# Second block of a two-block network: attention regrouped in units of two heads, with the top-k rounds between the units

## The reference, cut to what matters

```python
# 8 heads of 64 over 2 key/value heads; 8 index heads of 32; top 128 of the 512 keys per query
def block(i):                                   # a block of 128 queries; four of them
    rel = relu(einsum('bthd,bsd->bths', qi_b, ki))
    isc = einsum('bths,bth->bts', rel, wi_b * idx_scale)
    isc = where(causal, isc, -inf)
    _, sel = top_k(isc, 128)
    s = einsum(q, k[sel]) * 64 ** -0.5          # only the selected keys count
    s = where(valid, s, -inf)
    return einsum(softmax(s), v[sel])
short_conv = sc_b * causal_dwconv(sc_c * u, w_conv)      # three taps, width 512, from three products of h
```

## Time and profile before

| | before |
|---|---|
| median of three runs | 4325.65 us |
| lowest, highest | 4324.61, 4326.67 us |
| the profiled execution's own time | 4326.43 us |
| its span, first to last instruction | 4324.6 us |
| granted PE clock over the span, share of full | 0.958 |
| busy share PE, DVE, ACT, POOL | 92%, 44%, 36%, 29% |

### The profile page before, as it was taken

One profiled execution on the slowest core, in us unless ns is written; L12 is line 12 of the kernel. 1 busy time (PEld: TensorE's weight loads), 2 busy tenths in 40 slices (PEclk: granted clock), 3 DMA queues, 4 the chain that ended last, 5 costly groups with the idle time before them and its releaser, 6 DMA issues.

```text
span 4324.6 us, 60899 instructions
## 1 busy us (share of the span) xinstructions
PE 3957.5 (92%) x25712; PEld 3124.9 (72%) x25712; DVE 1884.7 (44%) x2939; ACT 1565.4 (36%) x2376; POOL 1250.8 (29%) x765
## 2 busy tenths in 40 slices
PE   7988899999999799999788899999997889999998
PEld 6955678888776568877566677788775667777886
DVE  3265332323345533436955422334368554223333
ACT  4356222222355533332353333333323433333332
POOL 2011422222111133332222235333322222354332
PEclk9998899999999899999899999999998999999999
DMA  5013133322111022221101022222211010222222
GB/s 200 30 56 137 59 112 103 108 102 101 61 49 61 20 81 88 98 69 68 54 30 36 22 78 98 81 88 102 83 61 52 30 36 22 83 93 78 98 93 73
DMA packets 61358, 323.55 MB, mean 75 GB/s; under 512 B 6176, under 2 KB 6304, under 8 KB 36256
## 3 DMA queue, kind: packets, MB, share of 16 engines
q1 hardware_dynamic: 61088, 319.65, 21.1%
HBM read 317.53 MB, written 2.10 MB: 74 GB/s over the span
## 4 chain that ended last, share of the span: by engine, by line
PE 77%; DVE 12%; ACT 5%; POOL 3%; issue 2%; DMA 1%; SPq 0%; DVEq 0%; ACTq 0%; POOLq 0%
PE ps L1509 51%; PE ps L704 3%; PE ps L724 3%; PE ps L2544 2%; PE ps L338 1%; PE ps L1008 1%; PE ps L3018 1%; PE ps L1043 1%; DMA adab<-in_wada 1%; DVE ar L2303 1%; DVE small L2299 1%; PE ps L2623 1%; PE ps L1023 1%; PE ps L1025 1%; PE ps L2636 1%
## 5 line engine op out<-in xcount | busy, mean ns | idle before, releaser
L1481 POOL TENSOR_TENSOR PWL<-ring,PWH 128x1024 fp32r<-128x1024 f32 (+2 forms) x116 | 267.1, 2303 | 715.7 <-ACT PWH L1467 715.7
L1888 DVE SCALAR_TENSOR_TENSOR ftmp<-ps,vec,ftmp 128x511 f32<-128x511 f32 (+2 forms) x440 | 301.8, 695 | 356.1 <-ACT ftmp L1842 231.4
L1467 ACT ACTIVATE PWH<-ring 128x1024 fp32r<-128x1024 f32 (+2 forms) x216 | 211.7, 982 | 513.5 <-PE ps L1509 485.7
L1481 POOL TENSOR_TENSOR WL<-ring,WH 128x1024 fp32r<-128x1024 f32 (+3 forms) x102 | 227.1, 2227 | 581.9 <-ACT WH L1467 565.4
L1467 ACT ACTIVATE WH<-ring 128x1024 fp32r<-128x1024 f32 (+3 forms) x160 | 158.8, 994 | 641.5 <-PE ps L1509 639.7
L1509 PE MATMUL ps<-FH,WH 128*128 128x512 f32 (+1 forms) x1056 | 332.0, 369 | 18.7 <-POOL FL L1682 14.6
L1509 PE MATMUL ps<-FL,WH 128*128 128x512 f32 (+1 forms) x1056 | 325.8, 363 | 0.0
L1509 PE MATMUL ps<-FH,WL 128*128 128x512 f32 (+1 forms) x1056 | 325.7, 363 | 0.0
L1481 POOL TENSOR_TENSOR PW3L<-ring,PW3H 128x1024 fp32r<-128x1024 f32 (+2 forms) x92 | 210.8, 2291 | 289.0 <-ACT PW3H L1467 288.7
L1474 DVE TENSOR_TENSOR PWL<-ring,PWH 128x1024 fp32r<-128x1024 f32 (+2 forms) x100 | 125.5, 1257 | 353.6 <-ACT PWH L1467 353.6
L1509 PEld LDWEIGHTS ps<-FH,WH 128*128 128x128 f32 x1056 | 178.0, 192 | 67.3 <-issue 28.1
(11 more groups left out here) (566 smaller groups left out, 10004.8 us busy)
## 6 DMA issues: line engine op xcount, KB each, us to landing
ring<-in_wup SPq DMA_DIRECT2D x88, 1024.0 KB, 4.8
adab<-in_wada SPq DMA_DIRECT2D x56, 512.0 KB, 5.5
ring<-in_wgate SPq DMA_DIRECT2D x24, 1024.0 KB, 4.8
ring<-in_wdown SPq DMA_DIRECT2D x24, 896.0 KB, 4.7
ring<-in_win SPq DMA_DIRECT2D x18, 1024.0 KB, 4.8
ring<-in_wout SPq DMA_DIRECT2D x16, 1024.0 KB, 4.9
ring<-in_wada SPq DMA_DIRECT2D x14, 1024.0 KB, 5.3
ring<-in_wdown SPq DMA_DIRECT2D x12, 1024.0 KB, 4.9
```

Of the source, the lines that this page charges most:

```text
L1467: e.activation(wh, view, ACT.Copy).then_inc(*whi_a.up(L, n))
L1481: e.tensor_tensor(wl, view, wh.bitcast(F32), SUB).then_inc(*wlo_g.up(L, n))
L1888: e.scalar_tensor_tensor(out=dst, in0=src, scalar=conv_cols(L, ch, a), in1=dst, op0=MUL, op1=ADD).then_inc(*(ffn_v.up(L, "tap", x, j, c) i ...
```

## The change

Part by part:

- Queries Q are scaled by -0.125 as they leave PSUM, so that scores are negative and the softmax needs the minimum, without a scaling of it.
- Index heads: no masked copies. A head's product uses its own 32 rows of PE (four heads in four banks). Their weighted sum is made by PE: POOL writes eight diagonal matrices of the heads' weights (`DI`), and eight 128x128 products add up in one bank (`weighted`). ACT copies the sum out.
- Attention units are 16, of two heads and one row group. The scores of the two heads use 64 rows of PE each, in two banks; mask, minimum and reciprocal are one DVE instruction for both. The exponentials aren't scaled; the turn is a product with a diagonal of the reciprocals (`diag2`, written by POOL). The values of the two heads use 64 columns each and are copied out together. The copies of the turned weights are ACT's, except one of two for the last row group.
- The convolution has one bank (6) instead of two, ACT copies all its products to SBUF, and it is cut in halves of 12 matmuls.
- `attend2_plan` writes out 25 slots; a row of it is (index scores, sum, unit, halves, rounds, selection): which index group, which sum, which unit, which halves of the convolution, which rounds and which selection stand in each. Rounds of one row group stand behind each other, beginning while the other groups' scores are still made, and go on between units 0 to 10; selections stand in the slots of units 3, 6 and 10.

`units_at(s)` gives a slot's unit u, the one before it, t = u-1, and v = u-2. ACT's order in a slot is: the weight split of an even half, the copy of the index sum, the relus, the two exponentials of u, the weight copies of t, the copy of the convolution's product when an odd half has ended it, the copy of v's result. POOL's is: the eight diagonals at the first scores of a row group, the two diagonals of t (they wait for its reciprocal), the low part of the weights of an even half. In `masked(u)` DVE adds the mask to the two heads' scores from PSUM and takes the minimum; `conv` is the product, the three taps and the last product of the convolution.

```diff
-                e.tensor_copy(x, bank(p % 2)).then_inc(*lin_v.up(L, p))
+                if P_Q <= p < P_K:
+                    e.tensor_scalar(x, bank(p % 2), -0.125, None, MUL).then_inc(*lin_v.up(L, p))
+                else:
+                    e.tensor_copy(x, bank(p % 2)).then_inc(*lin_v.up(L, p))
...
+        def attend2_plan():
+
+
+            rows = [((1, 0), 0, None, 1, {}, 0), ((1, 1), 0, None, 1, {}, 0), ((2, 0), 1, None, 1, {}, 0), ((2, 1), 0, None, 1, {1: 3}, 0),
+                    ((3, 0), 2, None, 1, {1: 3}, 0), ((3, 1), 0, None, 1, {1: 2, 2: 2}, 0), (None, 3, None, 1, {1: 2, 2: 2}, 0)]
+            rounds = [{1: 2, 2: 2}] * 3 + [{2: 2}] + [{2: 2, 3: 2}] * 2 + [{3: 2}] + [{3: 3}] * 3 + [{3: 1}] + [{}] * 7
+            for s in range(18):
+                rows.append((None, 0, s if s < 16 else None, (2, 1, 2, 1, 2, 1, 2, 2, 1, 1, 1, 1)[s] if s < 12 else 0, rounds[s],
+                             {3: 1, 6: 2, 10: 3}.get(s, 0)))
...
         def tensor_attend2(e, w, L):
+            def index(qi, j):
...
+                for r in range(4):
+                    rows = slice(32 * r, 32 * r + 32)
+                    e.matmul(bank(r)[:, 0:n], QI[rows, j, qi * 128:qi * 128 + 128], KI[rows, 0, 0:n], start=True,
+                             stop=True).then_inc(*idx_mm.up(L, qi, 4 * j + r))
+
+            def weighted(qi):
...
+                for h in range(8):
+                    w.wait_ge(idx_a.at(L, "relu", qi, h))
+                    mm = e.matmul(isc_bank(qi)[:, 0:n], DI[:, h, :], relu_buf(h)[:, 0:n], start=h == 0, stop=h == 7)
+            def conv_half(y):
+                x, h = divmod(y, 2)
...
+                w.wait_ge(whi_a.at(L, n), low_ready(L, n))
+                if x:
+                    w.wait_ge(idx_a.at(L, "conv", x - 1))
+            def scores(u):
...
+                w.wait_ge(soft_v.at(L, u - 2, "masked") if u >= 2 else idx_a.at(L, "relu", 3, 7))
+                for a in range(2):
+                    rows = slice(64 * a, 64 * a + 64)
+                    mm = e.matmul(scores2(u)[:, a, 0:n], Q[rows, jt, qi * 128:qi * 128 + 128], KK[rows, kv, 0:n], start=True, stop=True)
+            def turn(u):
+                w.wait_ge(diag_g.at(L, u))
+                for a in range(2):
+                    w.wait_ge(soft_a.at(L, u, "exp", a), weights_taken(L, u - 1, a) if u else idx_a.at(L, "isc", 3 if a else 2))
+                    for b in range(ATT2[u][0] + 1):
+                        mm = e.matmul(bank(4 + a)[:, b * 128:b * 128 + 128], E2(u)[:, a, b * 128:b * 128 + 128], diag2(u)[:, a, :],
+                                      start=True, stop=True)
+            def values(u):
...
+                for b in range(qi + 1):
+                    for a in range(2):
+                        mm = e.matmul(bank(7)[64 * a:64 * a + 64, 0:128], VT[:, b, c:c + 64], weights2(u, a)[:, b * 128:b * 128 + 128],
+                                      start=b == 0, stop=b == qi)
+            for s, (sc, acc, _, halves, _, _) in enumerate(PLAN2):
+                u, t, v = units_at(s)
+                if acc:
+                    weighted(acc)
+                if sc:
+                    index(*sc)
+                if u is not None:
+                    scores(u)
+                for y in halves[0:1]:
+                    conv_half(y)
+                if t is not None:
+                    turn(t)
+                for y in halves[1:]:
+                    conv_half(y)
+                if v is not None:
+                    values(v)
...
         def vector_attend2(e, w, L):
+            for s, (sc, acc, _, halves, rounds, sel) in enumerate(PLAN2):
+                u, t, v = units_at(s)
+                if t is not None:
+                    w.wait_ge(soft_a.at(L, t, "exp", 1))
+                    e.reciprocal(stat2(t)[2], stat2(t)[1]).then_inc(*soft_v.up(L, t, "inv"))
...
+                if u is not None:
+                    masked(u)
+                for y in PLAN2[s - 1][3] if s else ():
+                    if y % 2:
+                        conv(y // 2)
+                for qi, it in rounds:
+                    largest(qi, it)
+                if sel:
+                    selection(sel)
+                if t is not None and ATT2[t][0] == 3:
+                    w.wait_ge(turn_mm.at(L, t, 0), pv_mm.at(L, t - 2))
+                    e.tensor_copy(weights2(t, 0), bank(4)).then_inc(*wt_v.up(L, t, 0))

```

More of the change, by code:

```diff
@@ L2101, in gpsimd_turned @@
             pipeline([unit(p, *u) for p, u in enumerate(turned_units(L))])
[L2104 to L2112, removed]
-        def conv_bufs(ft):
-            return tmp2(14 + 2 * (ft % 2)), tmp2(15 + 2 * (ft % 2))
@@ L2117, in conv_fed @@
[L2117 to L2159, removed]
@@ new lines, in program, with relu_buf, isc_bank, conv_of @@
+        DI = hcf[:, 1024:2048].rearrange("p (h c) -> p h c", h=8)
+        ATT2 = [(qi, jt) for qi in range(4) for jt in range(4)]
+        def relu_buf(h):
+            return tmp2(6 + h)
+        def isc_bank(qi):
+            return bank(4 + qi % 2)
+        def conv_of(x):
+            return x // 3, (2, 0, 1)[x % 3]
+        def conv_bufs(ft):
+            return tmp2(14 + 2 * (ft % 2)), tmp2(15 + 2 * (ft % 2))
+        def conv_to(x):
+            ft, nm = conv_of(x)
+            return Y2[:, 4 + ft, :] if nm == 1 else conv_bufs(ft)[0 if nm == 2 else 1]
@@ new lines, in attend2_plan @@
+        def attend2_plan():
[5 more added lines that the diff above has]
+                             {3: 1, 6: 2, 10: 3}.get(s, 0)))
+            out, h, done = [], 0, {1: 0, 2: 0, 3: 0}
+            for sc, acc, u, halves, rnd, sel in rows:
+                todo = []
+                for i in range(max(rnd.values(), default=0)):
+                    for qi in sorted(rnd):
+                        if i < rnd[qi]:
+                            todo.append((qi, done[qi]))
+                            done[qi] += 1
+                out.append((sc, acc, u, list(range(h, h + halves)), todo, sel))
+                h += halves
+            assert h == 24 and all(x == 16 for x in done.values()), (h, done)
+            return out
@@ new lines, in program, with units_at, E2, weights2 @@
+        PLAN2 = attend2_plan()
+        def units_at(s):
+            first = next(i for i, x in enumerate(PLAN2) if x[2] == 0)
+            return [u if 0 <= u < 16 else None for u in (s - first, s - first - 1, s - first - 2)]
+        def E2(u):
+            return ar[:, 16472 + 1024 * (u % 2):17496 + 1024 * (u % 2)].rearrange("p (a c) -> p a c", a=2)
+        def weights2(u, a):
+            return tmp2(10 + 2 * (u % 2) + a)
+        def diag2(u):
+            return ar[:, 21592 + 256 * (u % 2):21848 + 256 * (u % 2)].rearrange("p (a c) -> p a c", a=2)
@@ L2345, in unit @@
-                yield 1
-                yield 1
-                w.wait_ge(turn_mm.at(L, u))
-                if u >= 2:
-                    w.wait_ge(pv_mm.at(L, u - 2))
-                e.tensor_copy(tmp2(6 + u % 2)[:, 0:n], bank(3 + u % 2)[:, 0:n]).then_inc(*wt_v.up(L, u))
-                yield 1
-            conv = vector_conv(e, w, L, (0, 1, 2))
-            among_scores(scores(), conv)
-            among_largest(largest(), conv)
-            first = selection()
-            next(first)
@@ L2358, in vector_attend2 @@
[L2358 to L2381 removed]
+                    w.wait_ge(soft_a.at(L, u - 8, "exp", 1))
```

319 lines of the change are left out of this document (147 added, 172 removed).

## The result

| | before | after |
|---|---|---|
| median | 4325.52 us (4 runs, 4324.61 to 4326.67) | 4288.94 us (4 runs: 4283.99, 4284.46, 4293.43, 4295.02) |
| profiled execution, its span | 4326.43, 4324.6 us | 4284.46, 4282.2 us |
| granted PE clock over the span | 0.958 | 0.961 |

The ratio is 0.9916, 95% interval 0.9899 to 0.9933: faster by 36.6 us. The forecast was 4285. The time is right; several of the reasons for it are not, as the trace shows.

What follows compares the result with a forecast made beforehand. The prediction had neither DVE nor PE full throughout, with DVE leading nearly all of slots 0 to 11 after the change. Stage 39.6 + 113.6 + 5 + 3 = 161.2 us against 181.8 and 182.1; 4326.4 - 41.5 = 4285 us, range 4252 to 4320.

Steps and rivals of the forecast that it cites:

- DVE's spread bounds the gain: Whole stage: neither DVE nor PE full throughout before; after, DVE leads nearly all of slots 0 to 11, 83.6 us.
- First part: Seven slots without units: PE works 38.8 us, first matmul 0.8 us in, DVE half idle; 39.6 us.
- Slots 0 to 11: Slots with units and rounds: DVE's 83.6 us plus its waits and the stalls beside POOL.
- The couplings: DVE's waits: 0.5 us for first scores, 4.0 at slot 0, 1.3 at slot 4, 1.7 at slot 11; 7.5 us.
- The stalls beside POOL: DVE's convolution products and selections beside POOL's weight splits: three stalls, 5 us a stage on top of unhindered times.
- Slots 12 to 15 with their clock loss: Last units, without rounds: a loop of 4.4 us a unit, 17.6 us, plus 3 us for PE at half clock.
- The tail: Behind the last unit: diagonal, turn, copy, values and copy with nothing beside; 4.9 us.
- The clock: PE stops 5.9 us at slot 10, then two slots at half speed: +3 us; gaps near 3 at slots 3 and 6 free.
- Signs named ahead: Trace signs: DVE busy near 118 us a stage, slots near 11 us at selections of groups 2 and 3, one half-clock stretch.
- Rival 3: Index path and units: PE tiles run in turn, not side by side; 4314 us, chance 0.05.
- rival 2: Units: DVE and PE wait alternately, hiding only half of PE's 81 us; stage 178, program 4318 us, chance 0.12.
- rival 4: Unit part: long DVE slots cost PE its clock throughout; stage 201, program 4365 us, slower than before, chance 0.07.
- Rival 1: Whole stage: no POOL stalls, no clock loss, slot 0's wait hidden; 150 to 153 us, program 4264, chance 0.14.

Runs made afterwards that it cites:

- e6: Changed kernel with only the plan edited: no rounds in the first seven slots, then 16 gathered slots of rounds, then units; stages 182.8 and 182.7 us.
- e1: Changed kernel with DVE's convolution step moved behind the rounds of its slot; stages 158.6 and 158.7 us, ratio to before 0.9905.
- e8: Changed kernel with the weighted sum over index heads moved from PE back to DVE; stages 165.5 and 165.5 us, ratio to before 0.9935.
- e2: Changed kernel with ACT's copy of a convolution product ahead of the exponentials where the finishing half is the slot's first; stages 162.5 and 162.6 us.
- e4: Changed kernel with all index heads on PE's rows 0 to 31, one row tile; stages 182.6 and 183.3 us, ratio to before 1.0002.
- e7: Changed kernel with both heads' scores on rows 0 to 63 and values of head 0 before those of head 1; stages 170.9 and 170.9 us.
- e3: Changed kernel with the edits of e1 and e2 together; stages 153.4 and 153.3 us, median 4260.7 us, ratio to before 0.9858.
- e10: e3 with more rounds of row groups 1 and 2 moved into the part without units; stages 150.7 and 150.7 us, ratio to before 0.9874.

## Why the prediction was right, and where not

- **That DVE's spread bounds the gain: right.** e6 gives back the whole 16 us a stage when the rounds are gathered again; e1 shows that what is taken from DVE in the units reaches the end nearly whole (100.7 to 92.2 us of busy time, 8.0 of the stage).
- **First part, 39.6 forecast, 43.0 measured.** Three terms make the 3.4 us. The first index product stood 1.7 us in, not 0.8. The six groups took 5.2 us from start to start, where the estimate was 3.9. Seven halves took 20.9, not 19.5: six of them 2.90 to 2.96 each instead of 2.78, and the last, behind the sum, 3.26. The longer halves are no sign of a change of tiling, which the prediction put at nothing "on an engine that is not the limit": in the kernel before a tile of 24 between products on all 128 rows took 5.74 us (3207.36 to 3213.10) instead of 5.57, which is as much more. PE is the limit of this part, though, and I had weighed its total of 121 us against DVE's 113, and not where each lies. The sum of the heads on PE cost little by that: 1.1 us a stage by e8.
- **Slots 0 to 11, 96.1 forecast with couplings and stalls, 97.7 measured** (2052.8 to the reciprocal at 2150.46). The couplings, 3.43 + 2.51 + 0.78 + 1.37 = 8.1 us, met the 7.5. Three came at slots 0, 4 and 11 as named; the 0.78 before the mask of unit 8 wasn't named, and the 0.5 for the first scores didn't come. The stalls beside POOL, put at 5, were five instructions and 8.9 us: this term was too small by 3.9. What was left of DVE's own work was 2.9 less than counted, although 2.7 us of it are rounds left over from the first part (the first mask stands at 2055.51). The last two errors nearly cancel.
- **Slots 12 to 15 with their clock loss, 20.6 forecast, 20.1 measured, by other terms.** DVE's timeline of the changed kernel at the end:

```profile
2153.11 1.23 DVE L2317 TENSOR_TENSOR ar<-ps,ar 128x1024 f32<-128x1024 f32 x1 [2.48 <-PE ps L2220]
...
2157.17 0.17 DVE L2375 RECIPROCAL small<-small 128x2 f32<-128x2 f32 x1 [0.99 <-ACT ar L2277]
...
2161.35 0.17 DVE L2375 RECIPROCAL small<-small 128x2 f32<-128x2 f32 x1 [0.99 <-ACT ar L2277]
...
2166.11 0.17 DVE L2375 RECIPROCAL small<-small 128x2 f32<-128x2 f32 x1 [0.99 <-ACT ar L2277]
...
2170.51 0.17 DVE L2375 RECIPROCAL small<-small 128x2 f32<-128x2 f32 x1 [0.99 <-ACT ar L2277]
```

  Reciprocals are 4.2 to 4.8 us apart, 4.45 on the mean, where 4.4 was forecast. The one before (2150.46 to 2157.17) is 6.71, with the wait of 2.48 for scores that stood behind a turn at half clock. The tail was 5.9, not 4.9.
- **The clock: the step that failed as it was put.** I had read from the earlier trace rows that gaps of 5.0 and 8.9 us bring 1.2 GHz, put one such stretch behind the gap at slot 10, and said of slots 3 and 6 that gaps near 3 cost nothing. The trace of the kernel before didn't bear that out. PE was at 1.2 GHz before the gap of 8.92 began, from 3.6 us into the one of 4.78 ahead of it (timeline of PE, then table by stretch):

```profile
3294.55 0.48 PE L2229 MATMUL ps<-cst,ar 128*128 128x128 f32 x1 [4.78 <-ACT ar L2264]
```

```profile
3292.00:3293.00 1.00, 0.00 (x0) 0.00 (x0) 0.41 (x4) 0.72 (x3) 0.00 (x0) 1.00 0.00 0
3293.00:3294.00 1.00, 0.00 (x0) 0.00 (x0) 0.90 (x5) 1.00 (x2) 0.13 (x1) 0.59 0.03 8
```

  In the changed kernel PE fell four times in the first stage, with gaps of 2.55, 4.31, 3.38 and, at slot 10, 4.77 us (and kept its clock in e2 after 1.78). The unit part has 0.92 granted, with PE at 1.2 GHz in several short stretches. Two parts of the changed kernel that hold such places, from the table by stretch:

```profile
2109.80:2119.80 10.00, 6.62 (x24) 5.36 (x23) 9.76 (x17) 1.75 (x6) 2.94 (x2) 0.72 0.13 29
2084.00:2094.00 10.00, 4.75 (x13) 3.76 (x14) 9.16 (x24) 2.46 (x8) 3.37 (x3) 0.66 0.18 54
```

  Much of it hid behind DVE. What reached DVE can be read at two places: 1.6 us before the mask of unit 1 (see e2), and 1.6 at slot 11, where a turn and values of twelve records each took 3.94 us at half clock (2147.99 to 2151.93) and 2.34 one slot on. A part of the wait of 2.51 before the mask of unit 5 comes on top. So my estimate is 3.2 to 5.7 us a stage: the 3 us were near, but for the falls that I had called free.
- **A reading that was wrong.** The prediction takes the 1.87 us of L2319 as an instruction with two SBUF inputs. It has one tensor and a scalar a row. That such an instruction is held too is under the hardware below.
- **Signs named ahead.** DVE's busy sum was 122.6 us a stage, not 118; the slots with selections of groups 2 and 3 took 12.6 and 11.2 us from reciprocal to reciprocal; and there were four stretches of clock 0.5, not one.
- **The total.** The stages gained 31.5 us where 41.5 was forecast, 10 us too much; the start of the first stage, 9.9 us earlier in unchanged code, made that up in the profiled execution. That is luck, and the 4285 for a median of 4288.9 was nearer than its working deserved. From the stages alone it would be 4326.4 - 31.5 - 1.1 = 4293.8. Rival 3 is excluded by e4 and e7, rival 2 by the couplings of 8 us, rival 4 by the 0.92. Rival 1's 150 to 153 us a stage come only with e3 and e10 (153.4 and 150.7), where edits take away most of the stalls and of slot 0's wait.

## What to carry to other kernels

Where two engines share a stage, set their work against each other part by part before adding it up: here the same instructions gave 166.6 or 182.8 us by their places alone. When an engine's instruction reads SBUF on DVE, look at what POOL does at that time and put a round of the largest, or an instruction that takes an input from PSUM, beside it. e1 tried this for the rounds; for PSUM it rests on the rows counted below. Compare the stretches that no edit touches as well, since a stage that gains 8 us can be followed by a recurrence that is 4 us longer at a lower granted clock.

## What the runs showed of the hardware

- A DVE product of two tensors in SBUF that started while POOL's split ran ended up to 0.6 us behind it: 2.90 and 2.87 us instead of 0.68. In e6 it was also a TENSOR_SCALAR with a single tensor input, from the timeline of that kernel:

```profile
2115.28 2.37 POOL L1481 TENSOR_TENSOR PWL<-ring,PWH 128x1024 fp32r<-128x1024 f32 x1 [0.68 <-ACT PWH L1467]
2115.32 2.61 DVE L2361 TENSOR_SCALAR ar<-ar,vec 128x512 f32<-128x512 f32 x1
```

  Unhindered it takes 0.49 us, less than the 0.69 of a reduction of that size. The Trainium skill, "SBUF — State Buffer", SBUF: two separate sides, gives the shared pair of ports to whichever starts first, for the whole instruction, and counts a DVE instruction in a mode that uses both ports among those that need it, beside those with two inputs in SBUF. The trace agrees for the products and for the SCALAR_TENSOR_TENSOR of the earlier trace rows; which mode the TENSOR_SCALAR ran in no row shows, and its 0.49 us only fit. MAX8 and the replacement were never hindered: in the stages of all thirteen profiles at least 285 and 270 of them start beside a split, and MAX8 takes 0.68 to 0.70 us for 512 elements there, the replacement 0.67 to 0.68. Six products of 512 elements with one operand in PSUM do so as well and take 0.68 to 0.69.
- Products on 32 rows of PE, eight records in four banks, took 0.71, 0.93 and 1.14 us for 256, 384 and 512 columns; in turn, on one tile, 1.99, 2.84 and 3.70.
- PE fell to 1.2 GHz during unbroken work, behind 3.70 us of products on a quarter of its rows (e4). It also fell with single gaps of 2.55 and 3.38 us in the changed kernel.
- The same unchanged matmuls ran at 0.233 us in one pass of the kernel before and at 0.228 in the others' first passes, at a granted clock of 1.00 in both; the later passes of the kernel before are at the faster rate. The cause stays open.
